# Queries, keys and probabilities of the forgetting heads turned by VectorE blocks and carried across partitions through DRAM

## The reference

```python
proj = rms_norm(x, norm1_g) @ w_in
# group A, 8 "fox" heads of 128 dims: q, k normalised by head, then
s_f = q @ k.T * 128**-0.5 + c_q - c_k          # c: running sum of log_sigmoid(forget logits)
o_f = softmax(where(key <= query, s_f, -1e30)) @ v
# group B, 8 "diff" heads: two softmaxes over 64-dim halves with rotary, p0 - lam * p1, then rms_norm
x = x + concat(o_f, o_d) @ w_out
u = causal_depthwise_conv3(rms_norm(x, norm2_g) @ w_up)      # 2 x 5504 features
out = x + (silu(gate) * val) @ w_down
```

## Time and profile before

| | |
|---|---|
| median of 3 runs | 1050.82 us (1050.48 to 1050.96) |
| profiled execution | 1050.86 us, its span 1049.1 us |
| PE busy | 1044.5 us |
| ACT busy | 778.1 us |
| DVE busy | 756.2 us |
| DMA | 211.33 MB, mean 201 GB/s |
| granted clock of PE | 1.000 |

### The profile page before, as it was taken

The page is one execution under the profiler, slowest core; times in us unless marked ns, Lnnn a source line. Parts: engine busy times, 40 slices in busy tenths (PEclk is TensorE's granted clock), DMA queues, the critical chain, the costliest instruction groups (busy, mean ns, idle before and its releaser), DMA issues.

```text
span 1049.1 us, 16985 instructions
## 1 busy us (share of the span) xinstructions
PE 1044.5 (100%) x5495; PEld 950.2 (91%) x5495; DVE 756.2 (72%) x1259; ACT 778.1 (74%) x1334; POOL 35.9 (3%) x43
## 2 busy tenths in 40 slices
PE   9999999999999999999999999999999999999998
PEld 8999999999999988888888888888889988888887
DVE  7788877777668764586776876777767678777664
ACT  7777666888856544879788788797887778758853
POOL 0101020000002210000000000000000000000000
PEclk9999999999999999999999999999999999999999
DMA  9655566565665666565565566665655766656664
GB/s 351 236 162 170 182 206 188 163 196 165 222 201 189 211 201 201 190 214 200 191 220 192 200 220 185 215 202 192 218 182 190 239 201 201 203 194 214 202 206 145
DMA packets 67083, 211.33 MB, mean 201 GB/s; under 512 B 9416, under 2 KB 10576, under 8 KB 66896
## 3 DMA queue, kind: packets, MB, share of 16 engines
q1 hardware_dynamic: 66880, 210.53, 61.6%
q10 hardware_dynamic: 144, 0.02, 0.0%
HBM read 208.42 MB, written 2.11 MB: 201 GB/s over the span
## 4 chain that ended last, share of the span: by engine, by line
PE 98%; ACT 1%; DMA 0%; DVE 0%; issue 0%; SPq 0%; DVEq 0%; ACTq 0%
PE ps L545 14%; PE ps L547 14%; PE ps L546 14%; PE ps L341 8%; PE ps L343 8%; PE ps L342 8%; PE ps L581 7%; PE ps L583 7%; PE ps L582 7%; PE ps L348 5%; PE ps L349 3%; PE ps L367 1%; PE ps L376 1%; DMA raw<-in_w 0%; PE ps L358 0%; ACT w_hi L629 0%
## 5 line engine op out<-in xcount | busy, mean ns | idle before, releaser
L1058 DVE TENSOR_TENSOR w_lo<-raw,w_hi 128x1024 fp32r<-128x1024 f32 (+1 forms) x406 | 463.5, 1148 | 228.4 <-ACT w_hi L629 226.0
L629 ACT ACTIVATE w_hi<-raw 128x1024 fp32r<-128x1024 f32 (+1 forms) x406 | 400.2, 988 | 183.6 <-PE ps L547 65.2
L545 PE MATMUL ps<-w_hi,xs 128*128 128x512 f32 (+1 forms) x704 | 263.5, 374 | 0.0
L546 PE MATMUL ps<-w_lo,xs 128*128 128x512 f32 (+1 forms) x704 | 263.4, 374 | 0.0
L547 PE MATMUL ps<-w_hi,xs 128*128 128x512 f32 (+1 forms) x704 | 263.4, 374 | 0.0
L341 PE MATMUL ps<-w_hi,xs 128*128 128x384 f32 (+1 forms) x512 | 172.8, 338 | 0.1
L342 PE MATMUL ps<-w_lo,xs 128*128 128x384 f32 (+1 forms) x512 | 167.0, 326 | 0.0
L343 PE MATMUL ps<-w_hi,xs 128*128 128x384 f32 (+1 forms) x512 | 167.0, 326 | 0.0
L545 PEld LDWEIGHTS ps<-w_hi,xs 128*128 128x128 f32 x704 | 133.1, 189 | 17.2
L547 PEld LDWEIGHTS ps<-w_hi,xs 128*128 128x128 f32 x704 | 133.1, 189 | 17.2
L546 PEld LDWEIGHTS ps<-w_lo,xs 128*128 128x128 f32 x704 | 133.1, 189 | 17.1
(11 more groups left out here) (158 smaller groups left out, 949.3 us busy)
## 6 DMA issues: line engine op xcount, KB each, us to landing
raw<-in_wrest SPq DMA_DIRECT2D x278, 512.0 KB, 3.8
raw<-in_win SPq DMA_DIRECT2D x117, 384.0 KB, 3.5
raw<-in_wrest SPq DMA_DIRECT2D x16, 384.0 KB, 3.0
xT<-in_xT SPq DMA_DIRECT2D x8, 256.0 KB, 7.8
xtok<-in_xtok SPq DMA_DIRECT2D x4, 512.0 KB, 13.2
raw_ahead<-in_w SPq DMA_DIRECT2D x5, 392.0 KB, 8.5
out<-x_tok SPq DMA_DIRECT2D x7, 256.0 KB, 4.4
raw_ahead<-in_win SPq DMA_DIRECT2D x3, 384.0 KB, 8.9
```

What stands on the lines that cost most here:

```text
L545: pe.matmul(o, xh, wh, start=(k == 0), stop=False, skip_group_check=True)
L546: pe.matmul(o, xh, wl, start=False, stop=False, skip_group_check=True)
L629: act.activation(slot(w_hi, s, w), slot(raw, s, w), ACT.Copy).then_inc(hi_ready, 1)
L1058: dve.tensor_tensor(slot(w_lo, s, w), slot(raw, s, w), f32(slot(w_hi, s, w)), ALU.subtract).then_inc(split_done, 1)
```

## The change

- Queries and keys of heads 9 to 15: the gains write them in an order of 32-column groups, DVE turns the blocks into `qnT` with an output step of four elements, SP stores `qnT` to DRAM (`qk_d`, 256 KB) and loads it in four DMAs of 64 KB, one for 32 partitions, into `qkT`. The copies of `move_qk` are gone, and TensorE's transposes for head 9 too. `block_scores` reads `qkT` with a step of four elements, after piece 6 in place of 5 (head 9: in place of 3).
- Probabilities of heads 9 to 14: `normalise` writes them to `pd` in groups, DVE turns them (`turn_p`, a new transpose of 128x384) at b = 7, SP stores them (`p_d`, 192 KB) and loads them in four DMAs into `pT`. TensorE's three transposes and ACT's copy are gone. `block_values` stands after piece 4 of the next frame, in place of piece 1.
- SP's loop over the pieces of these frames becomes an order written out, in which the stores and loads, each behind its wait, stand between the loads of weights.

```diff
-BLOCK_AT = dict(scores=5)
-MOVES = {1: (0, 5), 2: (5, 10), 3: (10, 15)}
-FOX1_AT = dict(turn=2, scores=3, probs=6, values=7)
+BLOCK_AT = dict(scores=6)
+QK0, P_STOP = H + 1, HEADS - 1
...
+    qk_d = nc.dram_tensor("qk_scratch", (P, 2 * S), F32, kind="Internal").ap()
+    p_d = nc.dram_tensor("p_scratch", (P, SROW), F32, kind="Internal").ap()
...
+        def blocks_counted(f):
+            return f - (QK0 - 1)
+        def pe_turned(f):
+            return f - max(0, min(f, P_STOP - 1) - (QK0 - 1))
...
-            with sp.Fori(17, IN_PIECES // RING) as i:
+            with sp.Fori(17, 2 * QK0 + 1) as i:
                 in_pieces(i)
+            def one_piece(g):
+                sp.wait_ge(split_done, g - RING + 1)
+                if g < IN_PIECES:
+                    sp.dma_start(slot(raw, g % RING, W1), win_d[(g - 8) * P:(g - 7) * P, :]).then_inc(raw_landed[g % RING], 16)
+                else:
+                    sp.dma_start(slot(raw, g % RING), wrest_d[(g - IN_PIECES) * P:(g - IN_PIECES + 1) * P, :]
+                                 ).then_inc(raw_landed[g % RING], 16)
+            def store_p(f):
+                sp.wait_ge(p_turned, blocks_counted(f))
+                if f > QK0:
+                    sp.wait_ge(pT_landed, 64 * blocks_counted(f - 1))
+                sp.dma_start(p_d, pdT[:]).then_inc(p_stored, 16)
+            def load_pT(f):
+                sp.wait_ge(p_stored, 16 * blocks_counted(f))
+                sp.wait_ge(pv_done, f - 1)
+                for j in range(4):
+                    src = p_d[:, j * 3 * 32:(j + 1) * 3 * 32].rearrange("(i r) c -> r i c", i=4)
+                    sp.dma_start(pT[32 * j:32 * (j + 1), :].rearrange("r (i c) -> r i c", i=4), src).then_inc(pT_landed, 16)
+            def store_qk(f):
+                sp.wait_ge(qk_turned, blocks_counted(f))
+                if f > QK0:
+                    sp.wait_ge(qk_landed, 64 * blocks_counted(f - 1))
+                sp.dma_start(qk_d, qnT[:]).then_inc(qk_stored, 16)
+            def load_qkT(f):
+                sp.wait_ge(qk_stored, 16 * blocks_counted(f))
+                sp.wait_ge(s_done, f - 1)
+                for j in range(4):
+                    src = qk_d[:, j * 4 * 32:(j + 1) * 4 * 32].rearrange("(i r) c -> r i c", i=4)
+                    sp.dma_start(qkT[32 * j:32 * (j + 1), :].rearrange("r (i c) -> r i c", i=4), src).then_inc(qk_landed, 16)
+            one_piece(8 * QK0 + 4)
+            one_piece(8 * QK0 + 5)
+            for f in range(QK0, HEADS):
+                one_piece(8 * f + 6)
+                if f > QK0:
+                    store_p(f - 1)
+                    load_pT(f - 1)
+                store_qk(f)
+                one_piece(8 * f + 7)
+                one_piece(8 * f + 8)
+                load_qkT(f)
+                for g in range(8 * f + 9, 8 * f + 14):
+                    one_piece(g)
+            one_piece(OUT0 + 6)
+            one_piece(OUT0 + 7)
...
+            def block_scores(f):
+                pe.wait_ge(qk_landed, f * 64 - 64 * (QK0 - 1))
+                turned = qkT[:].rearrange("p (u m n) -> p n m u", m=M, n=2)
+                for qb in range(M):
+                    last = pe.matmul(bank(B_S, qb * P, (qb + 1) * P), turned[:, 0, qb], turned[:, 1, 0:qb + 1], start=True,
+                                     stop=True, skip_group_check=True)
+                last.then_inc(s_done, 1)
+            def block_values(f, p):
+                pe.wait_ge(pT_landed, f * 64 - 64 * (QK0 - 1))
+                pe.wait_ge(mixlo_done, f - 1)
+                v = [qkv[:, (p * M + m) * QKV + 2 * HD:(p * M + m + 1) * QKV] for m in range(M)]
+                turned = pT[:].rearrange("p (i s t) -> p s i t", i=4, s=3)
+                pe.matmul(bank(B_O, 0, S), v[0], turned[:, 0:2], start=True, stop=False, skip_group_check=True)
+                pe.matmul(bank(B_O, P, P), v[1], turned[:, 2], start=False, stop=True,
+                          skip_group_check=True).then_inc(pv_done, 1)
...
                 if b == at["scores"]:
-                    scores(f, kind)
+                    if at is BLOCK_AT:
+                        block_scores(f)
+                    else:
+                        scores(f, kind)
...
-                    if spill and b == 0:
-                        prob_transposes(f - 1, "fox")
-                    if spill and b == 1:
-                        values(f - 1, par, "fox")
+                    if spill and b == 4:
+                        block_values(f - 1, par)
...
-            frame(H + 1, 1, "fox", FOX1_AT, trail=True)
-            frame(H + 2, 0, "fox", BLOCK_AT)
+            frame(H + 1, 1, "fox", BLOCK_AT, trail=True)
+            frame(H + 2, 0, "fox", BLOCK_AT, spill=True)
...
-            def move_qk(f, c):
-
-                i, jj = divmod(c, 4)
-                if c == 0:
-                    act.wait_ge(qk_turned, f - (H + 1))
-                src = qnT[32 * i:32 * (i + 1), :].rearrange("p (m n j t) -> p m n j t", m=M, n=2, j=4)[:, :, :, jj]
-                dst = qkT[32 * jj:32 * (jj + 1), :].rearrange("p (n m t) -> p m n t", n=2, m=M)[:, :, :, 32 * i:32 * (i + 1)]
-                last = act.activation(dst, src, ACT.Copy)
-                if c == 15:
-                    last.then_inc(qkT_ready, 1)
...
+                        if blocks:
+                            src, gain = [a.rearrange("p (j t) -> p j t", j=4) for a in (src, gain)]
+                            to = qn[:, p * 2 * M * w:(p + 1) * 2 * M * w].rearrange("p (j n t) -> p n j t", j=4, n=2 * M)[:, i]
+                        last = dve.scalar_tensor_tensor(out=to, in0=src, scalar=rs[:, i:i + 1], in1=gain, op0=ALU.mult,
+                                                        op1=ALU.mult)
...
-                dve.wait_ge(qkT_ready, f - 1)
-                dve.transpose(qnT[:], qn[:, p * 2 * M * HD:(p + 1) * 2 * M * HD]).then_inc(qk_turned, 1)
+                if not (isinstance(f, int) and f == QK0):
+                    dve.wait_ge(qk_stored, f * 16 - 16 * QK0)
+                turned = qnT[:].rearrange("p (j t c) -> p j c t", j=4, c=2 * M)
+                dve.transpose(turned, qn[:, p * 2 * M * HD:(p + 1) * 2 * M * HD].rearrange("p (j c t) -> p j c t", j=4, c=2 * M)
+                              ).then_inc(qk_turned, 1)
...
+                        src = to = s_sb[:, lo:lo + w]
+                        if blocks:
+                            src = src.rearrange("p (s j t) -> p s j t", j=4, t=32)
+                            to = pd[:].rearrange("p (j s t) -> p s j t", j=4, s=3)[:, qb:2 * qb + 1]
+                        last = dve.tensor_scalar(to, src, rl[:, qb:qb + 1], None, ALU.mult)
...
+            def turn_p(f):
+                dve.wait_ge(p_ready, f)
+                if not (isinstance(f, int) and f == QK0):
+                    dve.wait_ge(p_stored, f * 16 - 16 * QK0)
+                dve.transpose(pdT[:], pd[:]).then_inc(p_turned, 1)
...
+                        if p_blocks:
+                            turn_p(f)
+                        norm_apply(f + 1, 1 - p, next_kind, blocks=turn)
...
+                frame(f, 1 - f % 2, "diff", "diff" if f < H else "fox", DIFF_AT, trail=True, forget=f == 5,
+                      turn=f == H)
+            frame(H + 1, 0, "fox", "fox", BLOCK_AT, trail=True, turn=True, p_blocks=True)
+            frame(H + 2, 1, "fox", "fox", BLOCK_AT, turn=True, spill=True, p_blocks=True)
```

More of the change, by code:

```diff
@@ L145, in hybrid_layer_kernel @@
             pd = sa("pd", SROW)
+            pdT = sa("pdT", SROW)
             pT = sa("pT", SROW)
@@ L361, in scores @@
             def scores(f, kind):
-                pe.wait_ge(qkT_ready, f)
+                pe.wait_ge(qkT_ready, H + 1 if isinstance(f, int) and f == HEADS else f)
                 rows = [slice(0, P)] if kind == "fox" else [slice(c * DQK, (c + 1) * DQK) for c in range(2)]
@@ L660, in copy_qkT @@
             def copy_qkT(f, kind):
-                act.wait_ge(tp_done, H + 2 if isinstance(f, int) and f == HEADS else f)
+                act.wait_ge(tp_done, H + 1 if isinstance(f, int) and f == HEADS else f)
                 if kind == "fox":
@@ L757, in split_next, with frame @@
                 split_hi(f * 8 + (b + 4), b % RING, f * 2 + (2 + b // 4), w)
-            def frame(f, par, kind, next_kind, at=None, trail=False, last=False, forget=False, blocks=False, spill=False):
+            def frame(f, par, kind, next_kind, at=None, trail=False, last=False, forget=False, spill=False):
                 for b in range(8):
@@ L762, in frame @@
                         evacuate(f * 8 + 8, par, par)
[L763 to L768, removed]
+                        head_norm(f + 1, next_kind)
                     split_next(f, b, PW if last and b >= 4 else W1)
-                    if b == 7 and next_kind == "fox" and not blocks:
-                        head_norm(f + 1, next_kind)
                     if spill and b == 4:
                         mix_hi(f - 1, "fox")
[L774 to L780, removed]
```

(17 more changed lines are left out.)

32 lines of the change are left out of this document (12 added, 20 removed).

## The result

The changed kernel takes 1060.74 us (median of 5 runs, 1060.59 to 1063.86) against 1050.71 (1050.43 to 1050.96) before: 1.0102 times as long, interval 1.0091 to 1.0113. The forecast was 1054.1 in a range of 1048.8 to 1060.0: the direction was right, the size was not. The profiled execution took 1060.74 us, its span 1058.9.

What follows compares the result with a forecast made beforehand. TensorE, with 98% of the last chain, was taken as the bound, with SyncE's round setting the pace after the change: 5.1 plus 0.6 less 2.4 gives +3.3 us, forecast 1054.1, range 1048.8 to 1060.0.

Steps and rivals of the forecast that it cites:

- Strides: Block transpose and scores at a four-element step: forecast left 0; as rival, both take double time, 1058.3, chance 0.12.
- upper bound given: Twice the time for strided access: 0.64 us added for the block transpose, 0.66 us for the scores.
- The rival: Strides: 1.3 us in each of 7 frames, plus 0.7, less 2.4, is +7.4: 1058.3, chance 0.12.
- the cover before piece 3: Time between VectorE's split of piece 3 and TensorE's need of it: 1.05 us before, 0.05 afterwards.
- SyncE's round: Blocking stores and loads on SyncE delay piece 9 and row maxima: about 17.9 us against TensorE's 16.9; chance 0.46.
- The 0.85 us a frame of the sum: Late piece 9 delays row maxima 1.0 us, 0.15 covered; 0.85 passes on to piece 3's split, 6 frames, 5.1 us.
- The larger rules: Stride cost and the 0.85 don't add, since a later TensorE makes room for the late piece.
- TensorE's gain: Transposes removed: 0.33 us of P for six heads, 0.44 of queries and keys for head 9, 2.4 us.
- P's transpose in the hole: VectorE's new transpose of P, about 0.58 us, fits between T+1.97 and Newton at T+2.48, cost 0.
- the 0.1 us of piece 3: TensorE's loss before piece 3 with a cover of 0.05 us: 0.1 us in 6 frames, 0.6 us.
- Waits for pT and qkT: TensorE never waits for pT or qkT; loads hidden with 0.7 us to spare each.
- Transfers hidden: Rival: faster issues and stores, piece 9 in time, TensorE the bound throughout; -1.8 us, 1049.0, chance 0.34.

Runs made afterwards that it cites:

- e13b: Kernel before, with only the block transpose's writes and the scores' reads of heads 10 to 15 at a step of four elements: 1055.96 us.
- e14b: Kernel before, with the block transpose and scores of heads 10 to 15 at a step of two elements: 1050.92 us.
- e1: Changed kernel with block transpose and scores dense, all transfers and SyncE's order kept, columns mixed up: 1057.69 us.
- e5: e1 with the load of piece 9 issued ahead of the qkT loads: 1056.01 us.
- e10: e1 with other work on SyncE between each store and the loads waiting for it, values one piece later: 1055.67 us.
- e17: Kernel before with only P of heads 10 to 14 through DRAM, piece 7 ahead of pT loads, values ahead of scores behind piece 5: 1049.60 us.
- e15b: Kernel before plus the change's stores and loads as transfers nobody waits for: 1050.82 us.

## Why the prediction was wrong in size

- **The step that failed is "Strides"**: its price was put at 0, from the projection's moving operand, which alternates between two halves at full rate (in the kernel's `weave` they are 192 elements apart, not 384). That row doesn't carry over to a step of four elements. Measured: the block transpose +0.75 us (upper bound given: 0.64), the scores +0.77 (0.66). The upper bounds were nearly right, and the choice between the ends was wrong; the rival that took them, 1058.3, was given 0.12 and came nearest. The Trainium skill, Advanced Engine Details and Errata, section SBUF Cachelines, speaks of lines of 16 bytes and a penalty where each access meets another one; its statement that two hits on a line suffice agrees with e13b and e14b, where 16 bytes of step cost 0.77 and 0.58 us and 8 bytes 0.03 and 0.00. The penalty for another line at each access doesn't show in the earlier trace rows, though: there each access lies 768 bytes from the one before, next to the last but one, and 384 columns take 0.16 us. So neither the jump's length nor the change of line as such costs. That it is how seldom the same 16 bytes are met again fits all three, and is a reading of them, not tested apart.
- **The rival was 2.4 us short.** It had the transpose's time paid in every frame, and so it came, because the change itself takes the cover before piece 3 down to 0.05 us; 0.75 - 0.05 and the 0.1 make the stall of 0.81 in frames 10 and 11. With 1.05 us of cover it is free (e13b). Short were the scores (5.4 us, not 4.6), the stalls (5.5, not 5.2), and the out projection's wait of 1.0, which it doesn't name.
- **SyncE's round was there**, and the chain of e1 shows it. Piece 9 landed after 3.1 to 4.7 us, forecast 3.0, and the stores mostly sooner than put down (P 1.9 to 2.6 us against 2.4, queries and keys 2.1 to 2.3 against 2.6); of the 1.5 us between the rounds of 18.6 and 17.1, piece 9 makes 1.1 and P's store 0.5. In the mean the two errors cancel, 17.7 us against 17.9, and that execution's 1054.72 is near the 1054.1 forecast for a kernel whose step costs nothing. That is partly luck: e1's median is 1057.69, its runs go up to 1061.38, and what the round took in those no profile shows.
- **Slower, as forecast, but by another path.** The 0.85 us a frame of the sum were to come from piece 9. In the changed kernel SyncE's round holds the chain only in frames 11 and 15 (0.3 us of the stall in frame 12 and the out projection's 1.0 come from there); the other stalls and the scores hang on the step. So the direction doesn't confirm the forecast's mechanism.
- **The two don't add up.** The round of the stride (scores, maxima, exponentials, squares, transposes, split of piece 3) takes 18.5 to 18.6 us, that of SyncE 17.1 to 18.6. The changed kernel shows both; in frame 11 its chain that ended last is SyncE's:

```profile
208.04 2.55 DMA p_scratch<-pdT
...
212.46 2.18 DMA qk_scratch<-qnT
...
216.45 4.54 DMA raw<-in_win
...
282.58 1.84 DMA p_scratch<-pdT
...
290.25 5.75 DMA raw<-in_wrest
```

  In frame 13 it goes through scores, P's transpose, the block transpose and the split; in frame 15 (the last two lines) it is SyncE's again and ends in the out projection's wait. Therefore taking away the stride gives back only 3.0 us by the medians. e5 and e10, which take away the blocking too, give back 5, though their intervals overlap with e1's. "The larger rules" fits this.
- **TensorE's gain** of 0.33 us a head, P's transpose in the hole and the 0.1 us of piece 3 were right: e17 has the frame of 17.01 us that they give. Waits for pT and qkT: none in the changed kernel, as forecast, though e10 shows how near they were.
- **"Transfers hidden"** (1049.0) did not come; with the transfer of P alone and an order fitted to it, e17 gets near it (1049.60).

Open is what makes a load of 384 KB land now after 3.1 and now after 4.7 us in one place of the frame, and with it the spread of e1; and why the store of queries and keys from GpSimd's queue takes 4.9 us.

## What to carry to other kernels

When a change adds a step in an access pattern and no row of the trace has that step, read its price from the bounds, not from the nearest pleasant row; fold a layout change so that neighbours still share 16 bytes, as the step of two in e14b. Before work is taken off the bounding engine, look at what it covered: the cover before piece 3 was worth 0.7 us a frame as soon as somebody else became longer. And where two rounds of the same length run through a frame, undoing one shows only a part of its price (here 3.0 of 9.9 us): put each alone into the kernel before instead.

## What was not expected of the hardware

- A step of 4 fp32 elements doubles a VectorE block transpose's write (0.71 to 1.47 us for 128x512) and the moving read of an fp32 matmul (0.66 to 1.36 us for four matmuls); as stationary operand it takes the weight load from 190 to 332 ns, of which only 0.07 us reach the matmuls. A step of 2 is free (0.716 and 0.69 us).
- In e13b the strided transpose took 1.27 to 1.46 us, in the changed kernel 1.42 to 1.48.
- 65 DMAs with 6.0 MB more in these seven frames moved the time by 0.15 us, which is within noise, as long as nobody waited for them (e15b), though the loads of weights around them landed 0.4 us later in the median.
